# Page compression with operands split into a rounded high part and its rest, and the first pages asked for by three queues

## The reference, cut to what matters

```python
def _compress(x, w1, pe, w2):
    b, n, g, dh = x.shape
    xt = jnp.swapaxes(x, 1, 2).reshape(b * g, n, dh)
    h = lax.conv_general_dilated(xt, w1, (CMP_STRIDE,), 'VALID', dimension_numbers=('NWC', 'WIO', 'NWC'))
    h = jax.nn.gelu(h + jnp.einsum('rd,rdh->h', pe, w1)) @ w2
    return jnp.swapaxes(h.reshape(b, g, h.shape[1], dh), 1, 2)

# _nsa_sample: the cached rows come through the page table, 16 pages of 128 tokens per sample
kc_all = jnp.concatenate([pool_kc[page_table].reshape((b, past) + tail).astype(kc.dtype), kc], 1)
ck = _rms(_compress(kc_all, lp['cmp_k_w1'], lp['cmp_k_pe'], lp['cmp_k_w2']), lp['nsa_kcn'])
cv = _compress(vc_all, lp['cmp_v_w1'], lp['cmp_v_pe'], lp['cmp_v_w2'])
```

## Time and profile before

| what | value |
|---|---|
| median of 3 runs | 2545.19 us (2543.06 to 2546.51) |
| time of the profiled execution | 2545.03 us |
| its span, first to last instruction | 2543.4 us |
| PE busy in the span | 2368.4 us, 93% |
| DVE, ACT and POOL busy | 1144.4, 735.7 and 513.8 us |
| compression stage, first to last product | 233.8 to 394.4 us |

### The profile page before, as it was taken

One profiled execution on the slowest core, in us unless ns is written; L12 is line 12 of the kernel. 1 busy time (PEld: TensorE's weight loads), 2 busy tenths in 40 slices (PEclk: granted clock), 3 DMA queues, 4 the chain that ended last, 5 costly groups with the idle time before them and its releaser, 6 DMA issues. The chain is left out here.

```text
span 2543.4 us, 47485 instructions
## 1 busy us (share of the span) xinstructions
PE 2368.4 (93%) x19959; PEld 2070.9 (81%) x19959; DVE 1144.4 (45%) x2276; ACT 735.7 (29%) x1401; POOL 513.8 (20%) x377
## 2 busy tenths in 40 slices
PE   6998997999856999899989999999999999989998
PEld 3776884445534998888879999888999999989998
DVE  5532225555533445565654122355323332355665
ACT  4232124556612334222233110112111111123332
POOL 4001210000021232000012233321332323223332
PEclk8997898999976999999989999999999999999999
DMA  7335422101145141111112111241111111131221
GB/s 290 132 138 161 139 67 113 34 1 51 44 123 203 34 148 70 72 52 52 51 46 72 38 50 46 67 142 60 56 42 50 42 50 44 49 94 45 74 80 47
DMA packets 160709, 201.57 MB, mean 79 GB/s; under 512 B 14921, under 2 KB 144266, under 8 KB 156850
## 3 DMA queue, kind: packets, MB, share of 16 engines
q1 hardware_dynamic: 154866, 182.81, 22.3%
q0 software_dynamic: 5632, 15.74, 2.1%
HBM read 170.68 MB, written 31.99 MB: 80 GB/s over the span
## 5 line engine op out<-in xcount | busy, mean ns | idle before, releaser
L165 POOL CAST w_hi<-w_raw 128x1024 fp32r<-128x1024 f32 (+1 forms) x115 | 115.8, 1007 | 1300.5 <-DMA w_raw<-in_w_in 426.2
L173 PE MATMUL pP_u<-h_hi,w_hi 128*128 128x352 f32 x1056 | 340.9, 323 | 0.3 <-PEq L3044 0.3
L174 PE MATMUL pP_u<-h_lo,w_hi 128*128 128x352 f32 x1056 | 338.5, 321 | 0.0
L175 PE MATMUL pP_u<-h_hi,w_lo 128*128 128x352 f32 x1056 | 338.4, 320 | 0.0
L167 POOL TENSOR_TENSOR w_lo<-w_raw,w_hi 128x1024 fp32r<-128x1024 f32 (+1 forms) x115 | 275.5, 2396 | 9.2
L173 PEld LDWEIGHTS pP_u<-h_hi,w_hi 128*128 128x128 f32 x1056 | 198.1, 188 | 0.7 <-issue 0.6
L174 PEld LDWEIGHTS pP_u<-h_lo,w_hi 128*128 128x128 f32 x1056 | 198.5, 188 | 0.0
L175 PEld LDWEIGHTS pP_u<-h_hi,w_lo 128*128 128x128 f32 x1056 | 197.9, 187 | 0.0
L3332 DVE TENSOR_TENSOR conv<-conv,conv_sig 128x1056 f32<-128x1056 f32 x22 | 50.1, 2279 | 312.7 <-ACT conv_sig L3300 312.7
L173 PE MATMUL pP_d<-a_piece_hi,w_hi 128*128 128x352 f32 x528 | 173.4, 328 | 10.5 <-DVE a_piece_lo L3490 8.4
L3499 DVE TENSOR_TENSOR a_piece_lo<-aT,a_piece_hi 128x1408 fp32r<-128x1408 f32 (+1 forms) x71 | 135.8, 1917 | 93.0 <-ACT a_piece_hi L3428 93.0
(11 more groups left out here) (513 smaller groups left out, 5027.2 us busy)
## 6 DMA issues: line engine op xcount, KB each, us to landing
w_raw<-in_w_up SPq DMA_DIRECT2D x44, 512.0 KB, 4.1
ybT<-in_w_ada SPq DMA_DIRECT2D x9, 2048.0 KB, 8.0
w_raw<-in_w_in SPq DMA_DIRECT2D x30, 512.0 KB, 4.3
kv_ring<-in_pool_kv SPq DMA_DIRECT2D x80, 128.0 KB, 2.3
w_raw<-in_w_down SPq DMA_DIRECT2D x20, 512.0 KB, 3.5
pair_scratch<-hT SPq DMA_DIRECT2D x3, 2752.0 KB, 9.8
cx<-in_pool_c POOLq DMA_DIRECT2D x64, 128.0 KB, 3.1
cx<-in_pool_c SPq DMA_DIRECT2D x64, 128.0 KB, 3.0
```

The source lines that it names most:

```text
L165: engine.tensor_copy(hi, source).then_inc(done, 1)
L173: nc.tensor.matmul(out, w_hi, x_hi, start=start, stop=False)
L174: nc.tensor.matmul(out, w_hi, x_lo, start=False, stop=False)
L175: return nc.tensor.matmul(out, w_lo, x_hi, start=False, stop=stop)
```

## The change

The convolution of the eight sample jobs is made by three fp32r passes in place of fp32. ACT rounds the weights (`cw_hi_k`, `cw_hi_v`) and, twice per job, half of the job's pages (`cx_hi`); DVE subtracts and writes the rests (`cw_lo_k`, `cw_lo_v`, `cx_lo`). The high parts of the pages are laid out in the order in which the products read them, so that their 512 columns (two heads x 32 pages x 8 columns) are one run; the rests are written over the pages themselves and are read in runs of 8 elements. A job has then 8 steps x 2 halves x 3 passes = 48 products of 512 columns. The prompt's products stay fp32, but both heads go into one product of 132 columns: 16 products a job in place of 32.

The page table is loaded by SP in the stage before. The second weight matrix and the small loads move from SP to ACT's queue. The 32 first pages are asked for by SP (13), POOL (12) and ACT (7). The copies that turn the prompt's rows move from ACT to DVE. On ACT and DVE the gelu is cut in two pieces, with the rounding and the subtracts for later jobs between them. New tiles lie over old ones (`Pn`, `ybT`, the pages, the weights).

```diff
                 sp.dma_start(kn[:, :], A["norm_rows"]).then_inc(load, 16)
+                sp.dma_start(S["table"][:, :], A["page_table"]).then_inc(S["table_in"], 16)
                 for k, n in enumerate("kv"):
...
+        w1_v_at = start_of(nc)
         w1 = S["cw1"] + [sb("cw1_v", [128, 16, 128])]
+        old_rows = S["Pn"][:, :, :].rearrange("p a n -> p (a n)")
+        rounded = lambda n, s, at: nc.alloc_sbuf_tensor_at(n, s, F32R, offset=at)
+        w1_hi = [ctx.enter_context(nc.sbuf_tensor("cw1_hi_k", [128, 16, 128], F32R)), rounded("cw1_hi_v", [128, 16, 128], S["Pn_at"])]
+        w1_lo = [rounded("cw1_lo_k", [128, 16, 128], S["cw1_at"]), rounded("cw1_lo_v", [128, 16, 128], w1_v_at)]
+        x_hi = rounded("cx_hi", [128, 2, 4, 2, 32, 8], S["ybT_at"])
+        x_lo = rounded("cx_lo", [128, 2, 32, 2, 128], S["cx_at"])
...
-        pH = ps("pH", [128, 2, 2, 2, 256])
+        pH = ps("pH", [128, 2, 2, 512])
+        hidden_of = lambda j, hf, g, n: pH[:, j % 2, hf, g * n:g * n + n]
...
+        high_of = lambda m, g: x_hi[:, m % 2, :, g].rearrange("p i q c -> p q i c")
+        by_step = lambda x, g: x[:, :, g].rearrange("p q (i c) -> p q i c", i=4)
+        x_in = [[sem(f"cmp_x{b}_{q}") for q in range(3 if b == 0 else 2)] for b in range(2)]
+        first_of = [range(0, 13), range(13, 25), range(25, 32)]
+        landed = [[len(r) for r in first_of], [PAGES] * 2, [len(r) + PAGES * (r[-1] < 25) for r in first_of], [2 * PAGES] * 2]
...
-                for q in range(queue, 2 * PAGES, 2):
+                for q in first_of[queue] if grp == 0 else range(queue, 2 * PAGES, 2):
...
-                sp.dma_start(S["table"][:, :], A["page_table"]).then_inc(tab_in, 16)
-                sp.dma_start(w1[1][:, :, :], A["cw1_v"]).then_inc(w_in, 16)
-                for k, n in enumerate("kv"):
-                    sp.dma_start(w2[:, k], A[f"cw2_{n}"]).then_inc(w_in, 16)
-                sp.dma_start(kn[:, :], A["norm_rows"]).then_inc(w_in, 16)
                 pages(sp, 0)
...
-                    else:
-                        for q in range(2):
-                            pe.wait_ge(x_in[slot][q], 16 * PAGES * ((grp - 1) // 2 + 1))
                     if j >= 2:
                         pe.wait_ge(summed, j - 1)
                         pe.wait_ge(half, j - 1)
-                    for g in range(2):
+                    if grp == PROMPT:
                         for hf in range(2):
                             for i in range(8):
-                                if grp == PROMPT:
-                                    rhs = turned_prompt(S, kind)[:, g, i, :]
-                                else:
-                                    rhs = X[:, slot, :, kind, 64 * g + 8 * i:64 * g + 8 * i + 8]
-                                mm = nc.tensor.matmul(pH[:, j % 2, g, hf, 0:cols], w1[kind][:, 8 * hf + i, :], rhs,
-                                                      start=(i == 0), stop=(i == 7))
+                                mm = nc.tensor.matmul(pH[:, j % 2, hf, 0:2 * cols], w1[kind][:, 8 * hf + i, :],
+                                                      turned_prompt(S, kind)[:, :, i, :], start=(i == 0), stop=(i == 7))
+                        mm.then_inc(conv, 1)
+                        return
+                    if grp == 1:
+                        pe.wait_ge(w_low, kind + 1)
+                    for part in range(2):
+                        m = 2 * (j - 2) + part
+                        pe.wait_ge(x_low, 2 * m + 2)
+                        for i in range(4 * part, 4 * part + 4):
+                            at = slice(8 * (i % 4), 8 * (i % 4) + 8)
+                            hi = x_hi[:, m % 2, i % 4].rearrange("p g q c -> p (g q c)")
+                            lo = low_of(slot, kind, part).rearrange("p q g c -> p g q c")[:, :, :, at]
+                            for hf in range(2):
+                                mm = split_product(nc, pH[:, j % 2, hf, :], (w1_hi[kind][:, 8 * hf + i, :], w1_lo[kind][:, 8 * hf + i, :]),
+                                                   (hi, lo), i == 0, i == 7)
+                        if part == 0:
+                            mm.then_inc(first_half, 1)
                     mm.then_inc(conv, 1)
...
+                act.dma_start(w1[1][:, :, :], A["cw1_v"]).then_inc(w_in, 16)
+                for k, n in enumerate("kv"):
+                    act.dma_start(w2[:, k], A[f"cw2_{n}"]).then_inc(w_in, 16)
+                act.dma_start(kn[:, :], A["norm_rows"]).then_inc(w_in, 16)
+                act.wait_ge(tab_in, 16)
+
+                def first_pages(qs):
+                    for q in qs:
+                        load_pages(nc, act, S, A["pool_c"], q, X[:, 0, q].rearrange("p k c -> p (k c)"), x_in[0][2])
...
+                def weights_high(kind):
+                    if kind:
+                        act.wait_ge(w_in, 16 * 4)
+                        act.wait_ge(*S["nsa_out"][0])
+                        act.wait_ge(*S["nsa_out"][1])
                     else:
-                        nc.scalar.activation(S["cv"][0:nm - 1, seq, :], p2[0:nm - 1, 0:ns, :], ACT.Copy).then_inc(outc, 1)
-
-                for j in range(len(JOBS) + 2):
+                        act.wait_ge(S["cmp_k"], 16)
+                    nc.scalar.activation(w1_hi[kind][:, :, :], w1[kind][:, :, :], ACT.Copy).then_inc(w_high, 1)
+
+                def pages_high(m):
+                    j, half = 2 + m // 2, m % 2
+                    kind, grp = JOBS[j]
+                    slot = (grp + 1) % 2
+                    if kind == 0 and half == 0:
+                        for q, n in enumerate(landed[grp - 1]):
+                            act.wait_ge(x_in[slot][q], 16 * n)
+                    if m >= 2:
+                        act.wait_ge(*((conv, j) if half else (first_half, j - 2)))
+                    for g in range(2):
+                        nc.scalar.activation(high_of(m, g), by_step(rows_of(slot, kind, half), g), ACT.Copy).then_inc(x_high, 1)
+
+                first_pages(first_of[2][0:3])
+                weights_high(0)
+                first_pages(first_of[2][3:])
+                weights_high(1)
+                hidden(0)
+                sigmoid_of(0)
+                pages_high(0)
+                pages_high(1)
...
+                for j in range(1, len(JOBS) + 2):
+                    if 2 <= j < len(JOBS) - 1:
+                        pages_high(2 * j - 1)
                     if j < len(JOBS):
                         hidden(j)
                     if j >= 2 and JOBS[j - 2][0] == 0:
                         keys_turned(JOBS[j - 2][1])
                     if 1 <= j <= len(JOBS):
                         output(j - 1)
+                    if 1 <= j < len(JOBS) - 2:
+                        pages_high(2 * j)
+                    if j < len(JOBS):
+                        sigmoid_of(j)
+                    if 1 <= j <= len(JOBS) and JOBS[j - 1][0] == 0:
+                        root_of(JOBS[j - 1][1])
...
+                for kind in range(2):
+                    for g in range(2):
+                        dve.wait_ge(xp_t, 2 * kind + g + 1)
+                        nc.vector.tensor_copy(turned_prompt(S, kind)[:, g, :, 0:64], pX[:, g]).then_inc(xp_done, 1)
...
+                def weights_low(kind):
+                    dve.wait_ge(w_high, kind + 1)
+                    dve.wait_ge(conv, kind + 1)
+                    nc.vector.tensor_tensor(w1_lo[kind][:, :, :], w1[kind][:, :, :], w1_hi[kind][:, :, :].bitcast(F32),
+                                            ALU.subtract).then_inc(w_low, 1)
+
+                def pages_low(m):
+                    j, half = 2 + m // 2, m % 2
+                    kind, grp = JOBS[j]
+                    slot = (grp + 1) % 2
+                    for g in range(2):
+                        dve.wait_ge(x_high, 2 * m + g + 1)
+                        nc.vector.tensor_tensor(by_step(low_of(slot, kind, half), g), by_step(rows_of(slot, kind, half), g),
+                                                high_of(m, g).bitcast(F32), ALU.subtract).then_inc(x_low, 1)
+
+                weights_low(0)
+                gelu_of(0)
+                gelu_end(0)
+                for m in range(2):
+                    pages_low(m)
+                weights_low(1)
+                for j in range(1, len(JOBS) + 1):
+                    if 2 <= j < len(JOBS) - 1:
+                        pages_low(2 * j - 1)
                     if j < len(JOBS):
                         gelu_of(j)
+                    if 1 <= j < len(JOBS) - 2:
+                        pages_low(2 * j)
+                    if j < len(JOBS):
+                        gelu_end(j)
...
+                    S["cx_at"] = start_of(nc)
                     S["cx"] = sb("cx", [128, 2, 32, 2, 128], pages)
+                    S["ckn"] = sb("ckn", [128, 256], pages)
+                    S["cw1_at"] = start_of(nc)
                     S["cw1"] = [sb("cw1_k", [128, 16, 128], pages)]
+                    S["Pn_at"] = start_of(nc)
```

42 lines of the change are left out of this document (28 added, 14 removed).

## The result

| | before | after |
|---|---|---|
| time | 2545.85 us (2543.06 to 2551.39, 4 runs) | 2523.86 us (2520.52 to 2526.15, 4 runs) |
| ratio | | 0.991, 95% interval 0.9898 to 0.9922 |
| profiled execution, span | 2545.03, 2543.4 us | 2520.52, 2518.9 us |
| first transpose at | 233.76 us | 229.34 us |
| from there to the first sample job | 31.86 | 22.57 |

The stage lost 22.8 us, the medians lie 22.0 apart. From here on I read the stage.

What follows compares the result with a forecast made beforehand. PE was taken to bound the stage, which lies wholly ahead of the attention behind a barrier. 8.6 + 22.1 - 4.1 - 0.4 = 26.2 us off 2545.0 gave 2518.8 us, own range 2512 to 2524, wider range 2511 to 2535.

Steps and rivals of the forecast that it cites:

- start of the sample jobs: PE begins its first sample job at 257.0 us and not at 265.62, 8.6 us gained.
- products: In the eight sample jobs, 48 products of 0.232 us replace 64 records a job, 22.1 us gained.
- key norm: PE waits 0.9 to 1.1 us for normed keys ahead of the transpose at each of four joints, 4.1 us lost.
- late pages: ACT's roundings wait for a later group's pages, 0.4 us lost, at two joints at most.
- I take nothing: No extra time for the rests' products reading runs of 8 elements; upper bound 3.2 us a job, 26 us in all.
- The first rival: Rests' products wholly at fp32's pace: gain only 4.3 us, 2541 us; partly slow lies between; chance 0.20, mostly partial.
- The chain: From mid-job, two roundings, the second subtract, then DVE's last gelu step to the norm's end: 6.5 us with handshakes.
- Issue does not limit it: DMA does: First pages: 5.4 MB at 303 GB/s take 17.8 us, last page lands at 253.5; loads are issued by about 248.
- the second: Rival: roundings and subtracts through runs of 8 take a third longer, 5.5 us, 2524 us; chance 0.12.
- the fourth: Rival: the subtract takes 3.62 us, DVE bounds the jobs, 24 us slower, 2569 us; chance 0.04.
- the third: Rival: DVE stretches POOL's page loads to 1.65 us, each late group 7.6 us later, 2529 us; chance 0.06.

Runs made afterwards that it cites:

- e2: Changed kernel, but all 128 products of the rests read the contiguous high parts instead; 2515.95 us, stage 136.90 us against 139.19.
- e5: Changed kernel, but products of the rests read runs of 8 with four different distances between runs, by step; 2522.82 us, stage 138.27 us.
- e9: Changed kernel, but three of four rests' products read parts of the high half, in runs 96, 128 or 256 B apart; 2515.80 us, stage 136.60 us.
- e6: Changed kernel, but POOL asks for ten of the 32 first pages in the stage before; 2521.91 us, stage 135.41 us.
- e10: e7 with POOL asking for five of the first pages in the stage before; 2514.20 us, stage 133.08 us.
- e4: Changed kernel, but SP and POOL ask for 16 first pages each and ACT for none; 2525.15 us, stage 143.71 us.
- e3: Changed kernel, but PE does the projection of the gelu ahead of the key transpose; 2522.40 us, stage 138.44 us.
- e7: e3, and ACT asks for 4 of the 32 pages of each later group, SP and POOL for 14 each; 2519.30 us, stage 135.76 us.

## Why the prediction was right, and which terms were mis-sized

2518.8 us were forecast, with 2511 to 2535 about it; 2523.86 were measured. The mechanism stood as told, one term was too large and one cost too high, and these two misses partly made up for each other.

| term | forecast | measured in the stage |
|---|---|---|
| start of the sample jobs | +8.6 us | +9.3 (31.86 - 22.57) |
| products | +22.1 | +16.1 (8 x 13.92 - 8 x 16 x 0.7445) |
| key norm | -4.1 | -2.1 (three joints, 0.69 longer each) |
| late pages | -0.4 | -0.4 (one joint) |
| sum | 26.2 | 22.8 with the first job, the tail and what lies between |

0.7445 us is the sum of the three means above, for the three passes of one step and half.

**The products** are the step that failed. "I take nothing" for the rests' reads was wrong: 0.040 us each over 0.232, 128 of them, 5.1 us. The reason given, that the runs leave no mark in fp32, did not carry over. The other two passes took 0.235 and 0.238, and not 0.232, which is the remaining 1.1 us; with 0.232 the sum is 22.3 and not 22.1. The first rival in its partial kind came true, then, with 5 of its 26 us; e2, e5 and e9 show that the cause is where the runs lie.

**The key norm.** The chain was right: in the changed kernel a half takes 24 products, 5.96 us, and PE waits 0.50, together 6.46; in e2 5.64 and 0.80, together 6.44; forecast were 6.5. The wait was smaller because the slow rests gave the chain longer cover, and there are three joints, not four: the last norm falls into the tail, where it stood before. A joint at which PE waits costs some 0.2 us more than its idle time: from the last product of the k job to the next job it took 1.74 us against 1.05 before, with 0.50 idle. At the joint behind the late pages it was 1.24 against 0.83, with 0.17 idle.

**The start.** The time was right to 0.7 us, and so was the reason, "Issue does not limit it: DMA does": e6 and e10 bear it out, and e4 only shows that issue limits it where two queues ask. Two figures in it were off. The 303 GB/s came out as an average of the whole start, but of 81 GB/s in the first 2 us and 353 in the next 16. And 6.0 MB and not 5.4 were moved until the last page landed, 18.9 us behind the first transpose (19.7 were forecast), because the first pages of the next group were asked for meanwhile. Prompt jobs of 6.06 and 3.8 us, not 7.0 to 7.2, changed nothing, since PE waits 7.38 us behind them.

**The other rivals.** Rounding took 1.05 and subtract 1.22 us, so the second and the fourth fall. That no row of DVE depends on more than the number of elements was misread, though: the earlier trace rows has the same subtract at 1.21 and at 3.62 us. For the third, POOL's issues while DVE subtracts without a pause (3.40 of 3.40 us in the stretch from 251.90):

```profile
251.88 0.54 POOL L716 DMA_DIRECT2D cx<-in_pool_c  x1 [0.61 <-issue]
253.02 0.54 POOL L716 DMA_DIRECT2D cx<-in_pool_c  x1 [0.60 <-issue]
254.16 0.54 POOL L716 DMA_DIRECT2D cx<-in_pool_c  x1 [0.60 <-issue]
```

They are 1.14 us apart, as in the earlier trace rows, so the third falls too. The Trainium skill ("SBUF — State Buffer", section "SBUF: two separate sides") tells of GpSimd's DMAs starving for descriptors beside VectorE operations in a two-port mode, and has one with two SBUF inputs block only a GpSimd operation that reads SBUF. The trace is in line with that: these two-input subtracts held up no issue.

## What to carry to other kernels

Price a cheaper pass by a row that reads its operand from the same places, not only by the same instruction form: here a third of the passes ran 17% slower because their runs lay 256 B and more apart. Where two waits stand one behind the other, taking away the first (e3) gains nothing until the second goes too (e7). A third queue helps until DMA itself is busy throughout: read DMA's share ahead of the last landing before you ask from more queues (e4, e6). And loads that are moved ahead of a barrier count at the barrier: ask when the last of them lands, not only when it is issued (e10).

## What the runs showed of the hardware that was not expected

- An fp32r product of 512 columns took 0.228 to 0.242 us when its moving row came in runs 32 to 128 B apart, or in 16 or 32 runs 1 KB apart, 0.244 with 32 runs 256 B apart, and 0.27 with 64 runs 256 and 768 B apart. The Trainium skill, "Advanced Engine Details and Errata", section "Memory Cachelines", says that lines of 16 bytes are at full performance where an access hits the same line again; a run of 8 numbers is two lines with four hits each, and by that rule all these forms would be alike. The last two are not.
- The granted clock in the prompt jobs: in the kernel before it stayed at 0.50, the lower level of 1.2 GHz, from 238 to 250 us, PE and its weight loads busy throughout. In the changed kernel it rose at 238.03 us, in the first prompt job: the mean over 233.20 to 239.20 us is 0.60, and from there to 244.50 it was at 1.00, the level of 2.4 GHz. What sets it off was not tried.
